# The head of a layered kernel: x loaded in column quarters, the first two weight units multiplied in parts of 128 rows

## The chip, the cores and the metric

One core of a Trainium2 chip runs the kernel. The metric is the device time of one execution in microseconds (us), lower is better; a time shown is the median of several executions.

## The reference

The input x is 256 tokens of width 1024 in 32-bit floats. Three layers with feed-forward blocks follow; this case concerns only how the first one begins:

```python
u = rms_norm(h, norm_mix_g[l])            # (x * rsqrt(mean(x*x) + eps)) * gain
z = u @ w_in[l]                           # [256, 1024] @ [1024, 5640]
qa, ka, va, qk_b, vb, ob, ib, fb, ga, gb = jnp.split(z, IN_SPLITS, axis=-1)
qa = rope(to_heads(qa, A_HEADS), pos)
...
i_pre = (ib + b_igate[l].astype(ib.dtype)).transpose(0, 2, 1)
f_pre = (fb + b_fgate[l].astype(fb.dtype)).transpose(0, 2, 1)
hb = mlstm_chunkwise(to_heads(qb, B_HEADS), to_heads(kb_, B_HEADS), to_heads(vb, B_HEADS), i_pre, f_pre)
```

The eight columns ib and fb (the gates) are kept in a small tensor of their own, `wif`.

## The kernel before

**Units.** All weights stream through three slots of `raw`, one unit of 1 MB at a time. A wide unit is 512 rows by 512 columns: four row blocks (k = 0..3) of 128 rows, each a [128, 512] piece of the slot. Two units make one 512-column stretch of the output. Units 0 and 1 give the columns of qa, units 2 and 3 (`KA`) those of ka, units 4 and 5 (`VA`) va; units 6 to 9 (`QKB`) are narrow ones (256 columns by 1024 rows) for the convolution.

**Each product three times.** A weight w is split into `whi` (ScalarE, a copy that rounds) and `wlo` = w - `whi` (VectorE). x is split likewise into `xhi` and `xlo`. A product is xhi*whi + xhi*wlo + xlo*whi, three matmuls accumulated in PSUM. ScalarE increments `hi_done` with each unit, VectorE `lo_done`; TensorE increments `unit_used` when it is through with one, which lets ScalarE overwrite the slot's `whi`. The queue on SyncE (SP) refills a slot of `raw` when `lo_done` says that it is free.

**x.** x lies with its tokens on the partitions and must be turned: TensorE transposes it in blocks of 128x128 into PSUM banks 4 to 7 (`turn_x`, line 1970), 2 blocks for each of the eight chunks c of 128 columns. ScalarE copies a chunk out times the gain (`turned_gain`, line 680) to `xhi`, VectorE makes `xlo` (line 1054). The factor rsqrt(mean) is applied later, when the results leave PSUM.

**The head, in order.** SP issues x's columns 0 to 511 (one transfer for each of the two row tiles, 256 KB each, `x_full[0]`), then unit 0 as 128 rows, 128 rows and 256 rows, then x's columns 512 to 1023, `wif`, unit 1 in halves, three small ones, and whole units from there on. TensorE runs `idle(8)` (matmuls on zeros, 16 passes), turns the first half of x (8 transposes), runs `idle(6)`, and then `wide_halves(0)`: for each half of a unit 4 matmuls high*high, 4 xlo*whi, 4 xhi*wlo. The second half of x is turned in the middle of unit 0. After unit 0 come the gates' 8 matmuls (line 2039, all of x against `wif`), and unit 1.

**The gates' small work.** VectorE adds the two parts of the gate products (lines 1273, 1275); after unit 1 TensorE selects and turns them (line 2048, `gate_ps` 3), VectorE applies bias and factor (lines 1336 to 1342, `gate_dve` 2), ScalarE takes exp and log (lines 819, 821, with a table load) and after these copies the results of units 0 and 1 out of PSUM (line 808). VectorE then rotates them (`rotate`, lines 1101 to 1105, two row tiles), makes unit 5's `wlo`, and builds the diagonal matrices `diag` (lines 1301 to 1309). TensorE waits for these (`gate_dve` 5) ahead of four matmuls at line 2067, which stand between unit 4 and unit 5.

Every engine works through its own instructions in the order in which they are written; only semaphores tie them together.

Of the kernel before, what the change touches and what calls it, by code (L numbers as in the profile page):

```python
# [15 lines left out]
P = 128  # L16
# [45 lines left out]
TURN_BANKS = {T_MIX: (4, 5, 6, 7), T_Y0: (4, 5, 2, 3), T_M0: (0, 1, 5, 7), T_M1: (0, 1, 5, 7)}  # L62
# [122 lines left out]
def build(nc, t, out):  # L185
# [7 lines left out]
    with ExitStack() as ctx:  # L193
# [154 lines left out]
        quarter_hi, quarter_full = sem("quarter_hi"), sem("quarter_full")  # L348
        half_full = [sem(f"half_full{u}") for u in range(2)]
        half_hi, half_lo = sem("half_hi"), sem("half_lo")  # L350
        x_full = [sem(f"x_full{h}") for h in range(2)]
# [46 lines left out]
        def _(sp):  # L398
# [41 lines left out]
            def half_unit(u, h, s):  # L440
                k = 4 * u + 2 * h
                sp.dma_start(raw[:, u, 1024 * h:1024 * h + 1024].rearrange("p (a b) -> p a b", a=2),
                             cols(w_in, k, 2, 0, 512)).then_inc(s, 16)

            for h in range(2):
                for r in range(RT):
                    v = slice(512 * h, 512 * h + 512)
                    sp.dma_start(res[:, r, v], t["x"][0, r * P:(r + 1) * P, v]).then_inc(x_full[h], 16)
                if h == 0:
                    for k, s in enumerate((quarter_full, half_full[0])):  # L450
                        sp.dma_start(raw[:, 0, 512 * k:512 * k + 512], w_in[P * k:P * k + P, 0:512]).then_inc(s, 16)
                    half_unit(0, 1, raw_full[0])
            sp.dma_start(wif[:, :, :], t["wif"]).then_inc(wif_full, 16)
            half_unit(1, 0, half_full[1])
            half_unit(1, 1, raw_full[1])
# [3 lines left out]
            wide(KA, w_in, 512)  # L459
# [175 lines left out]
        def _(act):  # L635
# [174 lines left out]
            for u in range(PROJ):  # L810
# [3 lines left out]
                if u < PROJ - 1:  # L814
                    hi(u + 3, u % 3)
# [180 lines left out]
        def _(dve):  # L996
# [251 lines left out]

            def lo_half(u, h):
                v = slice(1024 * h, 1024 * h + 1024)  # L1250
                dve.wait_ge(hi_done if h else half_hi, u + 1)
                dve.tensor_tensor(wlo[:, u, v], raw[:, u, v], whi[:, u, v], ALU.subtract)\
                    .then_inc(lo_done if h else half_lo, 1)

            dve.wait_ge(gcol_full, 16)
            dve.wait_ge(quarter_full, 16)
            dve.tensor_copy(whi[:, 0, 0:512], raw[:, 0, 0:512]).then_inc(quarter_hi, 1)
            turned_gain(T_MIX, N_MIX, 0, (0, 1))
            dve.wait_ge(quarter_hi, 1)
            lo_half(0, 0)  # L1260
            turned_gain(T_MIX, N_MIX, 0, (2, 3))
            lo_half(0, 1)
            for h in range(2):
                dve.wait_ge(x_full[h], 16 * RT)
# [32 lines left out]
            for u in range(PROJ):  # L1297
# [22 lines left out]
                if u < 7 and u != 4:  # L1320
                    lo(u + 3)
                elif 7 <= u < 19:
                    scores(u - 7)
# [7 lines left out]
                if u == 0:  # L1331
                    dve.wait_ge(rstd_ready, 2)
                    dve.wait_ge(bias_full, 48)
                    dve.wait_ge(gate_ps, 3)
                    for r in range(RT):
                        ins = dve.scalar_tensor_tensor(out=gates[:, r, :], in0=ps[:, 4, 8 * r:8 * r + 8],
                                                       scalar=rstd[:, r:r + 1], in1=bif[:, :], op0=ALU.mult, op1=ALU.add)
                    ins.then_inc(gate_dve, 1)
                    dve.wait_ge(gate_dve, 1)
                    dve.scalar_tensor_tensor(out=rh(0), in0=f_pre, scalar=-1.0, in1=f_pre, op0=ALU.mult, op1=ALU.max)\  # L1340
                        .then_inc(gate_dve, 1)
                    link(dve.tensor_scalar(rh(72), f_pre, 0.0, None, ALU.min))
# [309 lines left out]
        def _(pe):  # L1652
# [316 lines left out]
            idle(8)  # L1969
            def turn_x(half):  # L1970

                pe.wait_ge(x_full[half], 16 * RT)
                for b in (2 * half, 2 * half + 1):
                    for c in (2 * half + b, 2 * half + b + 2):
                        bank, a = turn_at(T_MIX, c)
                        for r in range(RT):
                            ins = pe.transpose(ps[:, bank, a + P * r:a + P * r + P], res[:, r, P * c:P * c + P], ident)
                    ins.then_inc(tr_ps, 1)

            def wide_halves(u):  # L1980

                for h in range(2):
                    ks = (2 * h, 2 * h + 1)
                    if u == 0 and h == 0:
                        pe.wait_ge(quarter_hi, 1)
                    else:
                        pe.wait_ge(hi_done if h else half_hi, u + 1)
                    for k in ks:
                        pe.wait_ge(xhi_done, KC * T_MIX + 4 * u + k + 1)
                        if u == 0 and k == 1:  # L1990
                            pe.wait_ge(half_hi, 1)
                        for r in range(RT):
                            pe.matmul(ps[:, r, :], x(4 * u + k, P * r, P)[0], w(u, 512 * k, 512)[0],  # L1993
                                      start=u == 0 and k == 0, stop=False)
                    for r in range(RT):
                        for k in ks:
                            if r == 0:
                                pe.wait_ge(xlo_done, KC * T_MIX + 4 * u + k + 1)
                            pe.matmul(ps[:, r, :], x(4 * u + k, P * r, P)[1], w(u, 512 * k, 512)[0], start=False, stop=False)  # L1999
                    pe.wait_ge(lo_done if h else half_lo, u + 1)  # L2000
                    for r in range(RT):
                        for k in ks:
                            ins = pe.matmul(ps[:, r, :], x(4 * u + k, P * r, P)[0], w(u, 512 * k, 512)[1],  # L2003
                                            start=False, stop=u == 1 and k == 3)
                    if u == 0 and h == 0:
                        turn_x(1)
                ins.then_inc(unit_used, 1)
# [3 lines left out]
            idle(6)  # L2011
            tiles = 0
            for u in range(PROJ):
# [7 lines left out]
                if QKB <= u < VB:  # L2021
                    if free(tiles):
                        pe.wait_ge(*free(tiles))
                    narrow(u, u % 3, tiles % 4, turned=turned)
                    tiles += 1
                else:
                    if u < 2:
                        wide_halves(u)
                    else:
# [281 lines left out]
```

## Time and profile before

| | |
|---|---|
| median of 3 runs | 1347.59 us |
| lowest, highest | 1347.57, 1349.1 us |
| span of the profiled execution | 1345.7 us |
| TensorE busy (PE) | 1340.6 us |
| VectorE busy (DVE) | 1049.5 us |
| ScalarE busy (ACT) | 702.4 us |
| GpSimd busy (POOL) | 130.1 us |

The span runs from the first to the last instruction of one profiled execution; the page states no other time for that execution. The median is 1.9 us above the span. Busy times are sums over the span. Starts are counted from the span's start. PE is TensorE's matmuls, PEld its weight loads, SPq and ACTq are the instructions that issue transfers.

### The profile page before, as it was taken

Reading aid. Unit: us, or ns where it says so; the run is one execution under the profiler, and the core shown is the slowest. Engines: PE = TensorE matmul, PEld = TensorE weight load, DVE = VectorE, ACT = ScalarE, POOL = GpSimd, SP = SyncE. Lnnn points to the kernel's source line nnn. Section 1 sums busy time; section 2 is a strip of 40 time slices with the busy share of each in tenths; the row PEclk is TensorE's granted clock in tenths of the full one; section 3 lists DMA queues with packets and bytes.
Section 4 is the critical chain, followed back from the end, with each engine's and each line's share of the span. In section 5 each row is a group of like instructions: output and inputs, shape, how many; then the busy total and the mean of one; then the engine's idle time right before and its main releaser. Section 6 shows DMA issues by size and latency. Waiting matters only on the chain.

```text
span 1345.7 us, 18021 instructions
## 1 busy us (share of the span) xinstructions
PE 1340.6 (100%) x6497; PEld 1110.3 (83%) x6497; DVE 1049.5 (78%) x1802; ACT 702.4 (52%) x937; POOL 130.1 (10%) x158
## 2 busy tenths in 40 slices
PE   9999999999999999999999999999999999999999
PEld 8988888888888888887888888888888888888887
DVE  6994668878868877768778888698887888698775
ACT  5666446444464444577664444544445677644442
POOL 4042000020010000142000000000000432100000
DMA  9644455675555555554346555465556542455552
GB/s 278 211 161 149 166 169 190 235 262 200 200 165 198 199 194 191 172 182 144 126 145 230 187 187 188 156 219 187 187 187 207 169 157 95 149 197 196 200 199 90
DMA packets 108809, 246.30 MB, mean 183 GB/s; under 512 B 5112, under 2 KB 9636, under 8 KB 108624
## 3 DMA queue, kind: packets, MB, share of 16 engines
q1 hardware_dynamic: 106576, 240.19, 52.8%
q0 software_dynamic: 1744, 4.70, 1.2%
q8 instruction: 35, 0.57, 0.2%
q10 hardware_dynamic: 432, 0.66, 0.1%
q14 instruction: 22, 0.18, 0.0%
HBM read 244.45 MB, written 1.07 MB: 182 GB/s over the span
## 4 chain that ended last, share of the span: by engine, by line
PE 98%; DVE 1%; ACT 0%; issue 0%; POOL 0%; DVEq 0%
PE ps L1707 27%; PE ps L1655 17%; PE ps L1657 17%; PE ps L1656 17%; PE ps L1712 13%; PE ps L1904 1%; PE ps L1681 1%; PE ps L1958 1%; PE ps L1942 1%; PE ps L2227 0%; DVE wlo L1512 0%; PE ps L1966 0%; PE ps L1993 0%; PE ps L2003 0%; PE ps L1999 0%
## 5 line engine op out<-in xcount | busy, mean ns | idle before, releaser
L1707 PE MATMUL ps<-whi,xx 128*128 128x512 f32 x1600 | 379.2, 389 | 0.0
L1707 PEld LDWEIGHTS ps<-whi,xx 128*128 128x128 f32 x1600 | 300.4, 188 | 62.2
L1014 DVE TENSOR_TENSOR wlo<-raw,whi 128x2048 fp32r<-128x2048 f32 x120 | 274.7, 2289 | 63.9 <-ACT whi L651 62.5
L651 ACT ACTIVATE whi<-raw 128x2048 fp32r<-128x2048 f32 x120 | 229.1, 1909 | 88.4 <-PE ps L1712 88.4
L1212 DVE STREAM_TRANSPOSE sc<-sc 32x128 f32<-32x128 f32 x784 | 237.5, 303 | 11.7
L643 ACT ACTIVATE whi<-raw 128x2048 fp32r<-128x2048 f32 (+1 forms) x135 | 204.7, 1530 | 73.6 <-PE ps L1657 51.0
L1009 DVE TENSOR_TENSOR wlo<-raw,whi 128x2048 fp32r<-128x2048 f32 x75 | 171.2, 2289 | 45.9 <-ACT whi L643 45.5
L1655 PE MATMUL ps<-whi,hhi 128*128 128x512 f32 (+1 forms) x506 | 199.0, 393 | 0.0
L1712 PE MATMUL ps<-wlo,xx 128*128 128x512 f32 x800 | 197.6, 389 | 0.0
L1657 PE MATMUL ps<-whi,hlo 128*128 128x512 f32 (+1 forms) x506 | 197.0, 389 | 0.0
L1656 PE MATMUL ps<-wlo,hhi 128*128 128x512 f32 (+1 forms) x506 | 196.7, 389 | 0.0
L1655 PE MATMUL ps<-whi,xx 128*128 128x512 f32 x464 | 187.8, 405 | 0.3 <-DVE xx L1530 0.3
L1657 PE MATMUL ps<-whi,xx 128*128 128x512 f32 x464 | 181.7, 391 | 0.0
L1656 PE MATMUL ps<-wlo,xx 128*128 128x512 f32 x464 | 180.9, 390 | 0.0
L1712 PEld LDWEIGHTS ps<-wlo,xx 128*128 128x128 f32 x800 | 150.2, 188 | 31.1
L742 ACT ACTIVATE hhi<-sc 128x512 fp32r<-128x512 f32 x49 | 31.1, 634 | 193.4 <-DVE sc L1212 193.4
L1657 PEld LDWEIGHTS ps<-whi,hlo 128*128 128x128 f32 x506 | 95.0, 188 | 20.0
L1655 PEld LDWEIGHTS ps<-whi,hhi 128*128 128x128 f32 x506 | 95.1, 188 | 19.2 <-DVE hlo L1217 0.4
L1656 PEld LDWEIGHTS ps<-wlo,hhi 128*128 128x128 f32 x506 | 95.2, 188 | 18.7
L1657 PEld LDWEIGHTS ps<-whi,xx 128*128 128x128 f32 x464 | 87.1, 188 | 19.1
L1655 PEld LDWEIGHTS ps<-whi,xx 128*128 128x128 f32 x464 | 87.3, 188 | 17.3 <-issue 1.1
L1656 PEld LDWEIGHTS ps<-wlo,xx 128*128 128x128 f32 x464 | 87.5, 189 | 16.1
(286 smaller groups left out, 1165.8 us busy)
## 6 DMA issues: line engine op xcount, KB each, us to landing
raw<-in_ffn_gate_up SPq DMA_DIRECT2D x88, 1024.0 KB, 5.2
raw<-in_ffn_w_down SPq DMA_DIRECT2D x44, 1024.0 KB, 5.0
raw<-in_w_in SPq DMA_DIRECT2D x40, 1024.0 KB, 5.1
raw<-in_gate_up SPq DMA_DIRECT2D x22, 1024.0 KB, 5.2
raw<-in_w_out SPq DMA_DIRECT2D x12, 1024.0 KB, 4.9
raw<-in_w_down SPq DMA_DIRECT2D x11, 1024.0 KB, 5.0
raw<-in_w_mem_kv SPq DMA_DIRECT2D x4, 1024.0 KB, 5.2
raw<-in_w_proj_a SPq DMA_DIRECT2D x2, 1024.0 KB, 4.9
```

The source lines that it names most:

```text
L643: ins = act.activation(whi[:, slot, v], raw[:, slot, v], ACT.Copy)
L651: act.activation(whi[:, c % 3, :], raw[:, c % 3, :], ACT.Copy).then_inc(hi_done, 1)
L742: act.activation(hhi[:, par, :], hidT, ACT.Copy).then_inc(h_hi, 1)
L1009: dve.tensor_tensor(wlo[:, u % 3, v], raw[:, u % 3, v], whi[:, u % 3, v], ALU.subtract)\
L1014: dve.tensor_tensor(wlo[:, c % 3, :], raw[:, c % 3, :], whi[:, c % 3, :], ALU.subtract)\
L1212: ins = dve.transpose(dst[32 * a:32 * a + 32, :, b, :], src[32 * b:32 * b + 32, :, a, :])
L1655: pe.matmul(o, stat[0], mov[0], start=start, stop=False)
L1656: pe.matmul(o, stat[0], mov[1], start=False, stop=False)
L1657: return pe.matmul(o, stat[1], mov[0], start=False, stop=stop)
L1681: ins = pe.transpose(ps[:, bank, a:a + P], res[:, r, P * c:P * c + P], ident)
L1707: pe.matmul(ps[:, banks[r], :], x(4 * half + k, P * r, P)[part], whi[:, slot, 512 * k:512 * k + 512], start=half == 0 and k == 0 and part ...
L1712: ins = pe.matmul(ps[:, banks[r], :], x(4 * half + k, P * r, P)[0], wlo[:, slot, 512 * k:512 * k + 512], start=False, stop=half == 1 and k ...
```

## The change

x arrives in four column quarters (256 columns of both row tiles, one transfer of 256 KB each). Units 0 and 1 arrive in eight parts of 128 rows, two after each quarter of x. ScalarE and VectorE split each part by itself (`hi_part`, `lo_part`), each behind the chunk of x of the same number. TensorE turns a quarter of x (4 transposes) at a time and goes chunk by chunk: `high` (2 matmuls), `w_low` of the chunk before (2), `x_low` (2), with the next quarter turned ahead of `x_low` in chunks 1, 3 and 5. `idle(8)` becomes `idle(6)` (12 passes), `idle(6)` becomes `idle(2)` (4 passes). Units 2 and 3 arrive and are split in halves, and are multiplied by halves, three matmuls at a time. The gates' 8 matmuls move from behind unit 0 to behind unit 1, their selection (line 2048) from behind unit 1 to behind unit 2; on VectorE bias and factor of the gates come ahead of unit 4's `wlo` instead of behind unit 3's. ScalarE's square of x and its issue of the remaining constants (line 803) follow the last part of unit 1.

```diff
+            def x_part(q):
+                v = slice(256 * q, 256 * q + 256)
+                sp.dma_start(res[:, :, v], t["x"][0].rearrange("(r p) d -> p r d", p=P)[:, :, v]).then_inc(x_full[q], 16)
+
+            def w_part(u, k):
+                row = P * (4 * u + k)
+                sp.dma_start(raw[:, u, 512 * k:512 * k + 512], w_in[row:row + P, 0:512])\
+                    .then_inc(raw_full[u] if k == 3 else part_full[3 * u + k], 16)
+
+            def half_unit(u, h):
+                if u == 3:
+                    sp.wait_ge(lo_done, 1)
+                sp.dma_start(raw[:, u % 3, 1024 * h:1024 * h + 1024].rearrange("p (a b) -> p a b", a=2),
+                             cols(w_in, 4 * (u - KA) + 2 * h, 2, 512, 512))\
+                    .then_inc(raw_full[u % 3] if h else half_full[u - KA], 16)
+
+            for u in range(2):
+                x_part(2 * u)
+                w_part(u, 0)
+                w_part(u, 1)
+                x_part(2 * u + 1)
+                w_part(u, 2)
+                w_part(u, 3)
...
+            half_unit(KA, 0)
+            half_unit(KA, 1)
             sp.dma_start(bif[:, 0:BH], across(t["b_igate"][0])).then_inc(bias_full, 16)
             sp.dma_start(bif[:, BH:2 * BH], across(t["b_fgate"][0])).then_inc(bias_full, 16)
             sp.dma_start(cwr[:, :], t["conv_w"][0].rearrange("j (c p) -> (j c) p", p=P)).then_inc(bias_full, 16)
-            wide(KA, w_in, 512)
+            half_unit(KA + 1, 0)
+            half_unit(KA + 1, 1)
...
+            def hi_part(u, k):
+                act.wait_ge(raw_full[u] if k == 3 else part_full[3 * u + k], 16)
+                v = slice(512 * k, 512 * k + 512)
+                act.activation(whi[:, u, v], raw[:, u, v], ACT.Copy).then_inc(hi_done if k == 3 else part_hi, 1)
+
             def hi_half(u, h):
+                act.wait_ge(raw_full[u % 3] if h else half_full[u - KA], 16 * (u // 3 + 1) if h else 16)
+                if u == 3 and h == 0:
+                    act.wait_ge(unit_used, 1)
                 v = slice(1024 * h, 1024 * h + 1024)
-                if u == 0 and h == 0:
-
-                    v = slice(512, 1024)
-                act.wait_ge(raw_full[u] if h else half_full[u], 16)
-                act.activation(whi[:, u, v], raw[:, u, v], ACT.Copy).then_inc(hi_done if h else half_hi, 1)
+                act.activation(whi[:, u % 3, v], raw[:, u % 3, v], ACT.Copy).then_inc(hi_done if h else half_hi, 1)
 
             act.wait_ge(gcol_full, 16)
-            turned_gain(T_MIX, N_MIX, 0, (0, 1))
-            hi_half(0, 0)
-            turned_gain(T_MIX, N_MIX, 0, (2, 3))
-            hi_half(0, 1)
+            for c in range(KC):
+                act.wait_ge(tr_ps, c // 2 + 1)
+                act.activation(xhi[:, c, :], ps[:, 4 + c % 4, SEQ * (c // 4):SEQ * (c // 4) + SEQ], ACT.Copy,
+                               scale=gain_col(N_MIX, c)).then_inc(xhi_done, 1)
+                if c > 0:
+                    hi_part(c // 4, c % 4)
             act.wait_ge(wif_full, 16)
             act.activation(wifs[:, :, 0:8], wif[:, :, :], ACT.Copy).then_inc(wif_hi, 1)
-            act.wait_ge(x_full[0], 16 * RT)
-            act.wait_ge(x_full[1], 16 * RT)
+            for q in range(4):
+                act.wait_ge(x_full[q], 16)
             act.activation(xn[:, 0, :], res[:, 0, :], ACT.Square, scale=DM ** -0.5, accum_out=ss[:, 0:1]).then_inc(sq_done, 2)
-            turned_gain(T_MIX, N_MIX, 1)
-            hi_half(1, 0)
-            hi_half(1, 1)
             act.dma_start(cst[:, P:C_W], t["consts"][:, P:C_W]).then_inc(cst_full, 16)
-            hi(2, 2)
+            hi_half(KA, 0)
+            hi_half(KA, 1)
 
             def evac(n, dst, r, func=ACT.Copy):
 
@@ -811,7 +828,10 @@
                 if u == 17:
 
                     evac_pT(8)
-                if u < PROJ - 1:
+                if u == 0:
+                    hi_half(KA + 1, 0)
+                    hi_half(KA + 1, 1)
+                elif u < PROJ - 1:
                     hi(u + 3, u % 3)
...
+            for c in range(KC):
+                dve.wait_ge(xhi_done, c + 1)
+                dve.scalar_tensor_tensor(out=xlo[:, c, :], in0=ps[:, 4 + c % 4, SEQ * (c // 4):SEQ * (c // 4) + SEQ],
+                                         scalar=gain_col(N_MIX, c), in1=xhi[:, c, :], op0=ALU.mult, op1=ALU.subtract)\
+                    .then_inc(xlo_done, 1)
+                lo_part(c // 4, c % 4)
+            dve.wait_ge(wif_hi, 1)
+            dve.tensor_tensor(wifs[:, :, 8:16], wif[:, :, :], wifs[:, :, 0:8], ALU.subtract).then_inc(wif_lo, 1)
+            for q in range(4):
+                dve.wait_ge(x_full[q], 16)
             dve.tensor_tensor_reduce(out=xn[:, 1, :], in0=res[:, 1, :], in1=res[:, 1, :], scale=1.0 / DM, scalar=0.0,
                                      op0=ALU.mult, op1=ALU.add, accum_out=ss[:, 1:2]).then_inc(sq_done, 2)
-            dve.wait_ge(wif_hi, 1)
-            dve.tensor_tensor(wifs[:, :, 8:16], wif[:, :, :], wifs[:, :, 0:8], ALU.subtract).then_inc(wif_lo, 1)
-            turned_gain(T_MIX, N_MIX, 1)
-            lo_half(1, 0)
-            lo_half(1, 1)
-            dve.wait_ge(gate_ps, 1)
-            dve.tensor_copy(gate_t, ps[0:16, 4, 0:SEQ]).then_inc(gate_copied, 1)
-            dve.wait_ge(gate_copied, 1)
-            dve.tensor_tensor(gate_t, gate_t, ps[0:16, 4, SEQ:2 * SEQ], ALU.add).then_inc(gate_copied, 1)
-            lo(2)
+            lo_half(KA, 0)
+            lo_half(KA, 1)
+
+            def gate_sums():
+                dve.wait_ge(gate_ps, 1)
+                dve.tensor_copy(gate_t, ps[0:16, 4, 0:SEQ]).then_inc(gate_copied, 1)
+                dve.wait_ge(gate_copied, 1)
+                dve.tensor_tensor(gate_t, gate_t, ps[0:16, 4, SEQ:2 * SEQ], ALU.add).then_inc(gate_copied, 1)
+
+            def gate_inputs():
+                dve.wait_ge(rstd_ready, 2)
...
+                if u == 0:
+                    gate_sums()
+                    lo_half(KA + 1, 0)
+                    lo_half(KA + 1, 1)
+                if u == 1:
+                    gate_inputs()
+                if 0 < u < 7 and u != 4:
                     lo(u + 3)
...
-                if u == 0:
-                    dve.wait_ge(rstd_ready, 2)
-                    dve.wait_ge(bias_full, 48)
-                    dve.wait_ge(gate_ps, 3)
...
-            idle(8)
+            idle(6)
+
+            def turn_x(q):
+
+                pe.wait_ge(x_full[q], 16)
+                for c in (2 * q, 2 * q + 1):
+                    for r in range(RT):
+                        a = SEQ * (c // 4) + P * r
+                        ins = pe.transpose(ps[:, 4 + c % 4, a:a + P], res[:, r, P * c:P * c + P], ident)
+                ins.then_inc(tr_ps, 1)
+
+            def high(c):
+
+                u, k = c // 4, c % 4
+                if c == 0:
+                    pe.wait_ge(quarter_hi, 1)
+                elif k == 3:
+                    pe.wait_ge(hi_done, u + 1)
+                else:
+                    pe.wait_ge(part_hi, k + 3 if u else k)
+                pe.wait_ge(xhi_done, c + 1)
+                for r in range(RT):
+                    pe.matmul(ps[:, r, :], x(c, P * r, P)[0], w(u, 512 * k, 512)[0], start=c == 0, stop=False)
+
+            def x_low(c):
+
+                pe.wait_ge(xlo_done, c + 1)
+                for r in range(RT):
+                    pe.matmul(ps[:, r, :], x(c, P * r, P)[1], w(c // 4, 512 * (c % 4), 512)[0], start=False, stop=False)
+
+            def w_low(c):
+
+                u, k = c // 4, c % 4
+                pe.wait_ge(lo_done if k == 3 else part_lo, u + 1 if k == 3 else 3 * u + k + 1)
+                for r in range(RT):
+                    ins = pe.matmul(ps[:, r, :], x(c, P * r, P)[0], w(u, 512 * k, 512)[1], start=False, stop=c == KC - 1)
+                if k == 3:
+                    ins.then_inc(unit_used, 1)
+
...
+            idle(2)
+            for c in range(KC):
+                high(c)
+                if c > 0:
+                    w_low(c - 1)
+                if c in (1, 3, 5):
+                    turn_x((c + 1) // 2)
+                x_low(c)
+            w_low(KC - 1)
...
-                if u == 0:
+                if u == 1:
 
 
                     pe.wait_ge(wif_lo, 1)
@@ -2039,9 +2096,9 @@
                         ins = pe.matmul(ps[0:16, 4, :], wifs[:, k, :], xx[:, k, :, :].rearrange("p a b -> p (a b)"),
                                         start=k == 0, stop=k == KC - 1)
                     ins.then_inc(gate_ps, 1)
-                if u == 1:
                     pe.wait_ge(bias_full, 48)
                     pe.transpose(ps[:, 5, 0:32], cwr[:, :], ident[0:32, 0:32]).then_inc(gate_ps, 1)
+                if u == 2:
                     pe.wait_ge(cst_full, 16)
                     pe.wait_ge(gate_copied, 2)
                     for r in range(RT):
```

## Rows read from the trace of the kernel before

**Rows 1.** The page: chain of waits by engine, whole span.

```profile
PE 98%; DVE 1%; ACT 0%; issue 0%; POOL 0%; DVEq 0%
```

**Rows 2.** The chain of waits in time, 0 to 60 us: start, length, what.

```profile
1.05 3.79 PE ps L1966 x16
4.84 1.86 PE ps L1977 x8
8.95 0.91 PE ps L1999 x4
10.77 0.87 PE ps L1977 x8
```

**Rows 3.** Timeline of the head: start, length, engine, line, operation, idle before.

```profile
1.64 1.70 PE L1966 MATMUL ps<-pr 128*128 128x128 f32 x7
4.78 1.09 PE L1977 MATMUL ps<-cst,res 128*128 128x128 f32 x4
5.97 0.47 ACT L680 ACTIVATE xx<-ps,gcol 128x256 fp32r<-128x256 f32 x1 [2.81 <-PE ps L1977]
7.10 0.62 ACT L788 ACTIVATE whi<-raw 128x512 fp32r<-128x512 f32 x1
7.62 0.83 ACT L680 ACTIVATE xx<-ps,gcol 128x256 fp32r<-128x256 f32 x2
7.79 1.17 PE L1993 MATMUL ps<-whi,xx 128*128 128x512 f32 x4
7.82 1.23 DVE L1252 TENSOR_TENSOR wlo<-raw,whi 128x1024 fp32r<-128x1024 f32 x1
```

**Rows 4.** Transfers issued in three short windows: KB each, us from issue to landing.

```profile
res<-in_x SPq DMA_DIRECT2D x1, 256.0 KB, 3.1
cst<-in_consts ACTq DMA_DIRECT2D x1, 64.0 KB, 3.3
...
raw<-in_w_in SPq DMA_DIRECT2D x1, 256.0 KB, 4.1
...
raw<-in_w_in SPq DMA_DIRECT2D x1, 512.0 KB, 7.1
```

**Rows 5.** Timeline: when SP issued these.

```profile
0.74 0.86 SPq L448 DMA_DIRECT2D res<-in_x  x2
1.65 0.90 SPq L451 DMA_DIRECT2D raw<-in_w_in  x2
4.59 1.29 SPq L442 DMA_DIRECT2D raw<-in_w_in  x2
```

**Rows 6.** Busy time by windows, 0 to 6.5 us; at the end PEclk, DMA share, GB/s.

```profile
0.00:6.50 6.50, 5.45 (x24) 5.24 (x25) 0.61 (x3) 1.96 (x3) 0.32 (x6) 1.00 0.67 219
```

**Rows 7.** Timeline of the gates' small work, 21 to 37 us.

```profile
21.70 0.59 PE L2048 MATMUL ps<-cst,memT 16*128 16x8 f32 x4
24.72 0.35 DVE L1336 SCALAR_TENSOR_TENSOR small<-ps,rstd,bif 128x8 f32<-128x8 f32 x2
24.94 1.92 ACT L643 ACTIVATE whi<-raw 128x2048 fp32r<-128x2048 f32 x1 [2.45 <-DMA raw<-in_w_in]
25.20 0.17 DVE L1342 TENSOR_SCALAR small<-small 128x8 f32<-128x8 f32 x1
26.76 0.19 ACT L819 ACTIVATE small<-small 128x8 f32<-128x8 f32 x1
28.15 0.48 PE L1655 MATMUL ps<-whi,xx 128*128 128x512 f32 x1
28.37 1.25 ACT L808 ACTIVATE work<-ps,rstd 128x512 f32<-128x512 f32 x2
33.77 2.29 DVE L1009 TENSOR_TENSOR wlo<-raw,whi 128x2048 fp32r<-128x2048 f32 x1
36.91 2.50 DVE L1309 TENSOR_TENSOR turned_a<-cst,small 128x512 fp32r<-128x512 f32 x4
39.47 0.82 PEld L2067 LDWEIGHTS ps<-turned_a,hhi 128*128 128x128 f32 x4
```

More of the change, by code:

```diff
@@ L347, in build @@
         ident_full, warm_ready = sem("ident_full"), sem("warm_ready")
-        quarter_hi, quarter_full = sem("quarter_hi"), sem("quarter_full")
+        quarter_hi = sem("quarter_hi")
+        part_full = [sem(f"part_full{n}") for n in range(6)]
+        part_hi, part_lo = sem("part_hi"), sem("part_lo")
         half_full = [sem(f"half_full{u}") for u in range(2)]
         half_hi, half_lo = sem("half_hi"), sem("half_lo")
-        x_full = [sem(f"x_full{h}") for h in range(2)]
+        x_full = [sem(f"x_full{q}") for q in range(4)]
         raw_full = [sem(f"raw_full{s}") for s in range(3)]
@@ L1247, in _, with lo_part @@
             dve.memset(pr[:, 0, 0:P], 0.0).then_inc(warm_ready, 1)
+            def lo_part(u, k):
+                if u == 0 and k == 0:
+                    dve.wait_ge(quarter_hi, 1)
+                elif k == 3:
+                    dve.wait_ge(hi_done, u + 1)
+                else:
+                    dve.wait_ge(part_hi, k + 1 + 2 if u else k)
+                v = slice(512 * k, 512 * k + 512)
+                dve.tensor_tensor(wlo[:, u, v], raw[:, u, v], whi[:, u, v], ALU.subtract)\
+                    .then_inc(lo_done if k == 3 else part_lo, 1)
@@ L1249, in lo_half @@
             def lo_half(u, h):
+                dve.wait_ge(hi_done if h else half_hi, u + 1 if h else u - KA + 1)
                 v = slice(1024 * h, 1024 * h + 1024)
-                dve.wait_ge(hi_done if h else half_hi, u + 1)
-                dve.tensor_tensor(wlo[:, u, v], raw[:, u, v], whi[:, u, v], ALU.subtract)\
+                dve.tensor_tensor(wlo[:, u % 3, v], raw[:, u % 3, v], whi[:, u % 3, v], ALU.subtract)\
                     .then_inc(lo_done if h else half_lo, 1)
             dve.wait_ge(gcol_full, 16)
-            dve.wait_ge(quarter_full, 16)
+            dve.wait_ge(part_full[0], 16)
@@ L1257, in _ @@
             dve.tensor_copy(whi[:, 0, 0:512], raw[:, 0, 0:512]).then_inc(quarter_hi, 1)
[L1258 to L1264, printed above, removed]
+            for c in range(KC):
[4 more added lines that the diff above has]
+                lo_part(c // 4, c % 4)
@@ new lines, in gate_inputs @@
+            def gate_inputs():
+                dve.wait_ge(rstd_ready, 2)
+                dve.wait_ge(bias_full, 48)
+                dve.wait_ge(gate_ps, 3)
+                for r in range(RT):
+                    ins = dve.scalar_tensor_tensor(out=gates[:, r, :], in0=ps[:, 4, 8 * r:8 * r + 8],
+                                                   scalar=rstd[:, r:r + 1], in1=bif[:, :], op0=ALU.mult, op1=ALU.add)
+                ins.then_inc(gate_dve, 1)
+                dve.wait_ge(gate_dve, 1)
+                dve.scalar_tensor_tensor(out=rh(0), in0=f_pre, scalar=-1.0, in1=f_pre, op0=ALU.mult, op1=ALU.max)\
+                    .then_inc(gate_dve, 1)
+                link(dve.tensor_scalar(rh(72), f_pre, 0.0, None, ALU.min))
@@ L1330, in _ @@
                                       rbc0.unsqueeze(1).to_broadcast([P, 2, SEQ]), ALU.mult).then_inc(cin_done, 1)
-                if u == 0:
-                    dve.wait_ge(rstd_ready, 2)
-                    dve.wait_ge(bias_full, 48)
-                    dve.wait_ge(gate_ps, 3)
[L1335 to L1342, printed above, removed]
                 if u == 1:
@@ L1968, in _ @@
             pe.wait_ge(warm_ready, 1)
-            idle(8)
[L1970 to L1978, printed above, removed]
@@ L1980, in wide_halves @@
-            def wide_halves(u):
-                for h in range(2):
[L1983 to L1994, printed above, removed]
-                    for r in range(RT):
[L1996 to L2006, printed above, removed]
@@ new lines, in x_low @@
+            def x_low(c):
[5 more added lines that the diff above has]
+                pe.wait_ge(lo_done if k == 3 else part_lo, u + 1 if k == 3 else 3 * u + k + 1)
+                for r in range(RT):
+                    ins = pe.matmul(ps[:, r, :], x(c, P * r, P)[0], w(u, 512 * k, 512)[1], start=False, stop=c == KC - 1)
+                if k == 3:
+                    ins.then_inc(unit_used, 1)
@@ L2007, in wide_halves, with halved @@
+            def halved(u, banks):
+                for h in range(2):
+                    pe.wait_ge(lo_done if h else half_lo, u + 1 if h else u - KA + 1)
+                    for r in range(RT):
+                        for k in (2 * h, 2 * h + 1):
+                            ins = three(ps[:, banks[r], :], x(4 * (u - KA) + k, P * r, P), w(u % 3, 512 * k, 512),
+                                        u == KA and k == 0, u > KA and k == 3)
                 ins.then_inc(unit_used, 1)
@@ L2026, in _ @@
                 else:
-                    if u < 2:
-                        wide_halves(u)
-                    else:
+                    if 2 <= u < 4:
+                        halved(u, (tiles % 4, (tiles + 1) % 4))
+                    elif u >= 4:
                         wide(u, u % 2, (tiles % 4, (tiles + 1) % 4), (free(tiles), free(tiles + 1)),
```

20 lines of the change are left out of this document (3 added, 17 removed).

## The prediction
> **What bounds the kernel now.** I read the page's chain of waits first: 98% of it is TensorE, no other engine above 1% [rows 1]. The reader is to see that a matmul removed, or a pause of TensorE, counts at its full length, and that nothing later gives a pause back. The change alters no number of products (48 matmuls for units 0 and 1, 8 for the gates, 24 for each of units 2 and 3), so only three things can move the time: when TensorE starts on real products, whether it pauses once it has started, and at which clock it runs. I then read the chain in time and the timeline of the head. The first product starts at 7.79 [rows 3], and from there on products follow each other at 0.91 / 4 = 0.228 us [rows 2]. Before it lie 16 filler passes, 8 transposes, and fillers again [rows 2]. The most that an earlier start can bring is therefore a part of 7.79 us, and less than 2 us by the sum below, or 0.15% of the time.
>
> My sums are made against the span of 1345.7 us of the profiled execution; the median of the runs is 1.9 us above it, and I add the difference to the median.
>
> **The start.** x's first transfer lands 3.1 us after its issue at 0.74 [rows 4, 5]: 3.84. A column quarter has the same 256 KB in more and shorter pieces; I take 3.9, and bound it by 3.84 and by 4.7, where the second such transfer lands now. The identity matrix, issued at the same time by the other queue, lands after 3.3 us: 4.04 [rows 4]. That one is the later of the two. Fillers: passes start 0.213 apart ((1.70 - 0.42) / 6, a last one's length taken off [rows 3]); 12 of them from 1.05 end at about 3.8. So turning starts at about 4.15 (now 4.84 [rows 2]). Four transposes at 1.86 / 8 = 0.23 take it to 5.05, four filler passes to 5.9. Beside that ScalarE gets the first chunk 0.1 us after the transposes' modelled end, as now (the first four end at 4.78 + 1.09 = 5.87, ScalarE starts at 5.97 [rows 3]): 5.3, plus 0.47 = 5.75. The first part of unit 0, today issued at 1.65 as third 256 KB and there 4.1 us later [rows 4, 5], becomes the second transfer: about 4.8, its rounding about 5.3. First product at 5.9 instead of 7.79: **-1.9 us**. Bounds: 5.75 (the chunk) and 6.7 (if both transfers come a place late).
>
> **What then lies in TensorE's row.** Before, 8 transposes come after the first product, now 12. The 4 more cost 4 x 0.87 / 8 [rows 2] = **+0.45**. Each switch from transposes to products costs some 0.1 (the four products behind one take 1.17 [rows 3], where three steps of 0.228 and a last one of 0.39 make 1.07); there are 2 more: **+0.2**. The first two products fall into the stretch in which transposes still ran at half pace (0.23 against 0.11 each [rows 2]): **+0.4**, between 0 and 0.45.
>
> **New waits in the head.** In chunk 2 `high` needs `xhi` of chunk 2, which needs the quarter turned in chunk 1, and it needs `hi_part` of chunk 2, which stands behind that `xhi` on ScalarE although its weights landed long before. So from the transposes on there is a chain: 0.1 to wake ScalarE, 0.36 until its next instruction (two 0.47 copies of chunks take 0.83 together), 0.62 for a 512-column rounding [rows 3], about 0.05 to TensorE: 1.15 us from the transposes' modelled end. The only work between is `x_low` of chunk 1, 2 x 0.228, of which some 0.1 is already past by then. TensorE stands for 0.8 us. It is the same in chunks 4 and 6, since the turns stand in chunks 1, 3 and 5: 3 x 0.8 = **+2.4**. Bounds: 3 x 0.3, if rounding the part were not in the chain and only the 0.47 copy was, and 3 x 1.0. In chunks without a turn ScalarE needs about 0.36 + 0.55 per chunk against TensorE's 6 x 0.228 = 1.37, VectorE half of 1.23 [rows 3] and a 256-column operation, so both keep up. Landings are not in it: 256 KB now land per 0.7 to 1.1 us (unit 1's last half, the end of 3 MB, is there at about 5.3 + 7.1 = 12.4 [rows 4, 5]), while the last part is wanted only at about 18.
>
> Sum of the head: -1.9 + 0.45 + 0.2 + 0.4 + 2.4 = **+1.55 us** at the end of unit 1. Moving the gates' 8 matmuls costs nothing in TensorE's row. Their inputs are ready: ScalarE's copy of `wif` comes right after the last part of unit 1. Units 2 and 3 by halves: landed by 16, rounded by 22 and wanted at 23, free. SP waits for `lo_done` 1 (unit 0's slot free) ahead of unit 3's halves, as before; behind that wait stand only unit 4 and later, which must wait for later counts anyway. GpSimd's small loads start some 8 us later; nobody asks for them in this stretch.
>
> **The gates' small work.** Counted from the start of unit 3 (28.15), it runs now: selection at 21.70, bias and factor on VectorE 24.72 to 25.37, exp at 26.76, that is 1.39 ahead of unit 3; ScalarE could not be earlier since unit 4's rounding, late by its transfer, lasts until 26.86. Then table load and log, the two copies of the result until 29.62 (2.86 after exp), two rotations on VectorE up to 33.77, unit 5's `wlo`, and the diagonals from 36 to 39.41 [rows 7]. TensorE loads their first weight at 39.47, 0.06 later, where without a wait the load would stand about a tenth of a us earlier. This chain is just hidden: its cover is 0.1 us.
>
> Afterwards the selection comes behind unit 2. Its modelled end then lies about 0.3 before unit 3's start (the 0.36 us of the matmuls at line 2054 follow it); VectorE begins 0.1 later and needs 0.56 until ScalarE may start (24.72 to 25.28): exp at +0.4 instead of -1.39, **1.8 us later**. Unit 4's `wlo` (2.3) runs on VectorE meanwhile and is over before ScalarE's 2.86. Nothing in the rest of the chain gets shorter. TensorE reaches line 2067 at 11.5 after unit 3's start as before, the diagonals come 13.1 after it. With 0.1 of cover that makes **+1.65 us**. Bounds: 0, if some of VectorE's row from 29.6 on was waiting rather than working (I see no pause above 0.1 there), and 2.2. What stands behind it on VectorE moves with TensorE and so keeps its distance.
>
> **The sum.** +1.55 + 1.65 = +3.2 us: span 1348.9, time 1347.59 + 3.2 = **1350.8 us**, 0.24% slower. Its own range is 1349.9 to 1351.9.
>
> **The clock.** The page's PEclk reads 1.00 even for the first 6.5 us [rows 6], yet the transposes at 4.84 take twice as long as those at 10.77 [rows 2]: the engine ran at the lower of its levels (1.2 GHz) until shortly before 6.5, after 5.4 us of nearly gapless fillers, and at 2.4 GHz afterwards. The changed head has a pause of about 0.4 between fillers and transposes. The Trainium skill ("TensorE: Matmul & The Clock Gate", Part 1) says that the engine starts throttled, that activity releases it, and that the moment varies from run to run. This speaks against fewer fillers; the trace shows the late rise but not what a pause does to it.
>
> **Rivals.**
> (a) The clock rises late. From 5.9 to, say, 9.3 us products would take 0.43 instead of 0.23, by the ratio of the two rows of transposes. Half of 3.2 us is lost: +1.6, time 1352.4. For it: the new pause, and 4 fillers in place of 12. Against: the engine is busy for over 80% of the first 6.5 us in either order. 12%.
> (b) The chain of the gates stays hidden, because part of VectorE's row was slack. Then only the head counts: 1347.59 + 1.55 = 1349.1. Against it: 0.06 us between diagonals and weight load. 14%.
> (c) The head's waits do not appear, since ScalarE is woken earlier than I think or the rounding gets ahead: -0.85 for the head, +1.65 for the gates, time 1348.4. Against it: ScalarE's order is fixed in the code. 8%.
> (d) The other side, not slower: the earlier start carries through. The first product at 5.9 decides, and both chains fit under TensorE's work: from the turn to `high` within 0.35 us instead of 1.15 and the diagonals within 11.5 instead of 13.1. Price: -1.9 + 1.05 = -0.85, time 1346.7. It decides as soon as the hand-over is shorter than `x_low`. 4%.
> The forecast has 60%; 2% are left for other things.
>
> **Range and chances.** 0.2% is 2.7 us, about what a measurement of this kernel tells from no change. Slower by more means above 1350.3: most of the forecast's 60% (0.5) and (a) together, 0.61. Faster by more means below 1344.9, out of reach of an earlier start of 1.9 us: 0.02. The rest, 0.37, is within. For 8 in 10 I take the forecast, (a), and half of (b): 1349.0 to 1352.8.
>
> **What would show it.** First product (line of `high`) near 5.9; three pauses of TensorE of 0.8 us, each behind four transposes and two `x_low`, ended by ScalarE's rounding; no pause ended by a transfer. At the end of unit 1 TensorE is 1.5 us later than now. A pause of 1.6 us ahead of the diagonals' matmuls, ended by VectorE; from there on a constant distance of about 3.2 us. Wrong if the products of chunks 2, 4 and 6 follow without a pause, if the diagonals' weights load at once, or if the first products' pace stays at 0.43 beyond 7 us.

## The result, and the profile after

The change made the kernel slower. In the first session the median is 1352.96 us in 8 runs against 1348.03 us in 8 runs before: 4.9 us more. The ratio estimated from all runs is 1.0032, 95% interval 1.0024 to 1.0041, or 4.3 us. The forecast was 1350.8, 3.2 us more than 1347.59, with a range to 1352.8; its direction was right and its size too small. The median lies 0.2 above the top of that range, but the kernel before was 0.4 slower here than when the forecast was made. The 8 runs form two groups, three from 1350.58 to 1351.05 and five from 1352.90 to 1353.14. The profiled execution has a span of 1351.3 us against 1345.7.

The page's chain of waits by engine, kernel after:

```profile
PE 96%; DVE 2%; ACT 1%; issue 1%; DMA 0%; POOL 0%; ACTq 0%; DVEq 0%
```

It stood at 98% TensorE before [rows 1]. Two percentage points of 1351 us are not accurate enough for a sum, but they name the engines: VectorE and ScalarE now stand in the chain. The list of waits in the first 50 us shows where (who waited for whom: us in total, times, longest):

```profile
PEld ps L2031 <- ACT whi L798: 3.2, 3, 1.1
...
PE ps L2031 <- ACT whi L798: 1.9, 3, 0.6
...
PEld ps L2124 <- DVE turned_a L1355: 1.8, 1, 1.8
...
PE ps L2124 <- DVE turned_a L1355: 1.4, 1, 1.4
```

L2031 is `high`, L798 `hi_part`, L2124 the products with the diagonals (L2067 before). Three waits of equal kind, and one. The timeline of the kernel after at the first of the three:

```profile
9.76 1.05 PE L2017 MATMUL ps<-cst,res 128*128 128x128 f32 x4
...
10.47 0.81 PE L2037 MATMUL ps<-whi,xx 128*128 128x512 f32 x2
10.85 0.47 ACT L810 ACTIVATE xx<-ps,gcol 128x256 fp32r<-128x256 f32 x1 [3.90 <-PE ps L2017]
11.22 0.62 ACT L798 ACTIVATE whi<-raw 128x512 fp32r<-128x512 f32 x1
...
11.90 0.73 PE L2031 MATMUL ps<-whi,xx 128*128 128x512 f32 x2 [0.62 <-ACT whi L798]
```

Read it from the turn down: ScalarE copies the chunk 0.04 us after the transposes' modelled end (10.81), rounds the part from 11.22 to 11.84, and `high` starts at 11.90. Between lie only the two low products of 10.47. The other two pauses end at 15.97 and 20.07. The rounding had had its data for about 3 us: the part of the weights was issued at 2.68 and landed 5.3 us later, at 8.0 (ScalarE sat idle for 3.90 before the copy).

The start of the head, from the chain of waits in time (start, length):

```profile
0.74 3.53 DMA res<-in_x
4.41 1.08 PE ps L2017 x4
5.49 0.85 PE ps L2006 x4
6.34 1.06 PE ps L2031 x2
7.40 0.85 PE ps L2037 x2
8.26 0.85 PE ps L2031 x2
9.11 0.85 PE ps L2044 x2
9.96 0.87 PE ps L2017 x4
```

Two products take 0.85, nearly twice the 0.46 of before, and four transposes 0.87, where eight took as much before [rows 2]: TensorE stayed at 1.2 GHz up to about 10.4 us, against 6.5 before. PEclk prints 1.00 for 6.0 to 10.5 us too, so the clock must be read from the pace of equal instructions.

The gates' small work, answering to [rows 7]:

```profile
31.16 0.61 PE L2105 MATMUL ps<-cst,memT 16*128 16x8 f32 x4
31.91 0.36 DVE L1315 SCALAR_TENSOR_TENSOR small<-ps,rstd,bif 128x8 f32<-128x8 f32 x2 [3.36 <-PE ps L2105]
32.50 0.21 ACT L839 ACTIVATE small<-small 128x8 f32<-128x8 f32 x1 [2.57 <-DVE small L1319]
34.14 1.25 ACT L825 ACTIVATE work<-ps,rstd 128x512 f32<-128x512 f32 x2
39.53 2.29 DVE L1029 TENSOR_TENSOR wlo<-raw,whi 128x2048 fp32r<-128x2048 f32 x1
42.68 2.50 DVE L1355 TENSOR_TENSOR turned_a<-cst,small 128x512 fp32r<-128x512 f32 x4
```

The distances from exp to the copies and from unit 5's low part to the diagonals are as before. Only the start hangs on something else: VectorE idles 3.36 us until the selection, ScalarE 2.57 until VectorE. The products with the diagonals, in the timeline of the kernel before and in the chain in time of the kernel after:

```profile
39.63 1.09 PE L2067 MATMUL ps<-turned_a,hhi 128*128 128x512 f32 x4
```

```profile
45.23 1.20 PE ps L2124 x4
```

They start 5.6 us later. The last product before them starts at 43.42 in the kernel after, so the pause is 1.81 - 0.23 = 1.6 us. From 45.23 to the start of TensorE's last matmul it is 1303.1 us, against 1302.9 before: all but 0.1 to 0.2 us of the difference is made in the first 45 us.

### The profile page after: what moved, and what is told of

Read it like the earlier page. It is cut to its first block, busy times and chain, and to the rows that moved or that the text cites. A ratio compares the mean times of both kernels' runs of the same rounds, so it can differ in the third digit from the quotient of the medians.

```text
span 1351.3 us, 18017 instructions
## 1 busy us (share of the span) xinstructions
PE 1342.6 (99%) x6485; PEld 1109.4 (82%) x6485; DVE 1050.2 (78%) x1808; ACT 702.9 (52%) x942; POOL 133.3 (10%) x158
## 4 chain that ended last, share of the span: by engine, by line
PE 96%; DVE 2%; ACT 1%; issue 1%; DMA 0%; POOL 0%; ACTq 0%; DVEq 0%
PE ps L1747 27%; PE ps L1695 17%; PE ps L1697 17%; PE ps L1696 16%; PE ps L1752 13%; PE ps L1944 1%; PE ps L1721 1%; PE ps L1998 1%; PE ps L1982 1%; PE ps L2284 0%; DVE wlo L1552 0%; PE ps L2031 0%; PE ps L2044 0%; DMA res<-in_x 0%; PE ps L1908 0%
## 5 line engine op out<-in xcount | busy, mean ns | idle before, releaser
L656 ACT ACTIVATE whi<-raw 128x2048 fp32r<-128x2048 f32 (+1 forms) x133 | 200.9, 1525 | 69.6 <-PE ps L1697 55.2
```

Source lines behind the costliest of these rows:

```text
L656: ins = act.activation(whi[:, slot, v], raw[:, slot, v], ACT.Copy)
```

## The experiments

All were timed in several rounds beside the kernel before, in three further sessions; the changed kernel itself was timed again in the second of these alone. Of its fourteen runs seven form the lower group, 1350.6 to 1351.4 with a median of 1351.0; "the lower group" below means these. Each run has a profiled span, and the time is 1.7 to 1.9 us above it but for two runs, named below.

**Twelve fillers in the kernel before.**

```diff
-            idle(8)
+            idle(6)
```

> The kernel before with 12 filler passes ahead of the transposes instead of 16, so TensorE pauses for about 0.9 us between them (3.8 to 4.8); nothing else changes. Theory P (the pause among the fillers puts the clock's rise off): the transposes stay at 0.21 each and the first products run at 0.43, the rise comes well after 7 us, as in the changed kernel, and the time is 1 to 2.5 us above before. Rival Q (the moment of the rise is chance from run to run, whatever the fillers do): the profile may show either, and the runs of this kernel and of the kernel before are spread over the same two groups in about the same shares.

Median 1348.85 (11 runs from 1346.90 to 1349.49) against 1347.54 in 33 runs of before: ratio 1.0005, interval 0.9996 to 1.0014, which is not clear of no difference. The single runs say more. Three of its runs lie at or below 1347.55, like 17 of the 33 of before; eight lie at 1348.2 to 1349.5, where before has 2 of 33. Its profile:

```profile
4.72 1.94 PE L1977 MATMUL ps<-cst,res 128*128 128x128 f32 x8 [0.73 <-DMA res<-in_x]
6.45 2.34 PE L1966 MATMUL ps<-pr 128*128 128x128 f32 x12
8.55 0.71 PE L1993 MATMUL ps<-whi,xx 128*128 128x512 f32 x2
```

The twelve fillers (6.45) ran at half pace up to about 8.2 us and took 2.1 us in the chain, where they had taken 1.3; they themselves kept the first product back from 7.79 to 8.55, and the products with the diagonals start 0.8 us later than before (40.43). Theory P foresaw a rise after 7 us, which it got, and half-pace products, which this profile does not show. Q foresaw about the same shares; 8 of 11 against 2 of 33, in one session and with nothing else changed, speak clearly for P. They do not tell whether the pause or the smaller number of fillers does it.

**Only the gates' place moved, in the kernel before.** Products behind unit 1, selection behind unit 2, VectorE's order as in the change:

```diff
-                if u == 0:
+                if u == 1:
                     pe.wait_ge(wif_lo, 1)
...
+                if u == 2:
                     pe.wait_ge(cst_full, 16)
                     pe.wait_ge(gate_copied, 2)
...
```

> The kernel before with only the gates' work moved as in the change: 8 products behind unit 1, selection behind unit 2, bias and factor ahead of unit 4's low part. Theory: the diagonals come 1.8 us later against 0.1 us of cover, so TensorE pauses 1.4 to 1.8 us ahead of the diagonals' matmuls and the time rises by 1.6 us (0.12%). Rival (the pause in the changed kernel comes from the head, not from the gates' place): no pause there and no difference in time.

Median 1349.82 against 1347.54, 2.3 us more; ratio 1.0017, interval 1.0008 to 1.0026. From its list of waits:

```profile
DVE small L1326 <- PE ps L2049: 3.4, 1, 3.4
ACT small L819 <- DVE small L1330: 2.9, 1, 2.9
...
PEld ps L2068 <- DVE turned_a L1305: 1.8, 1, 1.8
```

The pause is the same 1.6 us as in the changed kernel (starts 39.98 and 41.79). So it belongs to the gates' place, not to the head. A second one of 0.4 us, not foreseen, appears between units 0 and 1: the gates' 8 products had covered ScalarE's rounding of unit 1's first half. Its timeline:

```profile
14.39 0.96 PE L1994 MATMUL ps<-whi,xx 128*128 128x512 f32 x3 [0.26 <-ACT whi L788]
```

A third part needs no wait. From the first product to the start of unit 3 it is 21.2 us, where it had been 20.4; without the pause of 0.4 another 0.4 is left. The selection and the small transpose ahead of it stood together behind unit 1, with one gap of TensorE in front of them; now they stand in two places, each with a gap. The prediction had put the move at nothing in TensorE's row.

**Quarters turned earlier, in the changed kernel.**

```diff
             for c in range(KC):
+                if c in (1, 3, 5):
+                    turn_x((c + 1) // 2)
                 high(c)
                 if c > 0:
                     w_low(c - 1)
-                if c in (1, 3, 5):
-                    turn_x((c + 1) // 2)
                 x_low(c)
```

> The changed kernel with each quarter of x turned ahead of the high products of chunks 1, 3 and 5, not behind the low products. ScalarE's chain (wake, copy of the chunk, rounding of the part) takes 1.15 to 1.25 us and then lies beside six products (1.37 us). Theory: the three pauses of 0.8 us go, 2.3 us less than the changed kernel. Rival (the parts' transfers or VectorE are just behind ScalarE): the pauses shrink, but 0.2 to 0.5 us is left at each, ended by another engine or a transfer, 1 us less in all.

Median 1348.38 (nine runs 1347.87 to 1348.52, two at 1350.0 and 1350.2): 2.6 us below the lower group of the changed kernel, which was timed in other sessions. The timeline of TensorE around the place of the first pause:

```profile
7.36 0.60 PE L2017 MATMUL ps<-cst,res 128*128 128x128 f32 x4
7.71 0.71 PE L2031 MATMUL ps<-whi,xx 128*128 128x512 f32 x2
8.26 0.62 PE L2044 MATMUL ps<-wlo,xx 128*128 128x512 f32 x2
8.72 0.63 PE L2037 MATMUL ps<-whi,xx 128*128 128x512 f32 x2
9.19 0.62 PE L2031 MATMUL ps<-whi,xx 128*128 128x512 f32 x2
```

There is no pause at any of the three places, so whatever stands behind ScalarE (VectorE, the parts' transfers) was ready in time. A pause costs a little more than its idle time. From one such `high` to the next, two chunks later, it is 3.22 us here (7.71 to 10.93) and 4.09 in the kernel of the next experiment but one (9.50 to 13.59, both at full pace): 0.87 for each pause, 2.6 for three.

**ScalarE rounds the part before it copies the chunk**, TensorE's order unchanged:

```diff
             for c in range(KC):
+                if c > 0:
+                    hi_part(c // 4, c % 4)
                 act.wait_ge(tr_ps, c // 2 + 1)
...
-                if c > 0:
-                    hi_part(c // 4, c % 4)
```

> The changed kernel with ScalarE rounding each part of the weights ahead of copying the chunk of x of the same number, instead of behind it; TensorE's order is as in the changed kernel. Theory: the 0.55 to 0.6 us of rounding leave the chain between turn and high product and only the copy (0.47) stays, so the three pauses of 0.8 us shrink to about 0.25 each, 1.6 us less than the changed kernel (1349.2 against 1350.8 in the lower group). Rival (VectorE's low parts or the weights' transfers stand right behind ScalarE): the pauses stay above 0.5 us, less than 1 us gained.

Median 1349.93; six runs from 1349.29 to 1350.22, three from 1351.45. The three gaps between starts shrink from 1.01 to 0.59 us, so each pause from 0.79 to 0.36, 1.3 us in all (0.3 us less than forecast). One of the six, 1350.22, has a span of 1347.7, so 2.5 us of its time lie outside the span, 0.7 more than in the others. What is left:

```profile
10.61 0.47 ACT L812 ACTIVATE xx<-ps,gcol 128x256 fp32r<-128x256 f32 x1 [2.60 <-PE ps L2017]
...
11.23 0.70 PE L2031 MATMUL ps<-whi,xx 128*128 128x512 f32 x2 [0.20 <-ACT xx L812]
```

`high` starts 0.15 us after the copy's end instead of 0.06 after the rounding's. Both instructions of ScalarE were in the chain, as the forecast had it.

**The gates' selection in the middle of unit 2**, in the changed kernel:

```diff
+                    if u == KA and h == 0:
+                        pe.wait_ge(cst_full, 16)
+                        pe.wait_ge(gate_copied, 2)
+                        for r in range(RT):
+                            sel = pe.matmul(ps[:, 4, 8 * r:8 * r + 8], ...)
+                        sel.then_inc(gate_ps, 1)
...
```

The selection behind unit 2 is left out in return.

> The changed kernel with the gates' selection between the halves of unit 2 instead of behind it. Exp on ScalarE then follows unit 4's rounding at about 30 instead of 32.5. Theory: the diagonals are there before TensorE wants them, the pause of 1.6 us ahead of their matmuls goes, 1.6 us less than the changed kernel. Rival (VectorE has too much work in that stretch, the chain of the gates only looks like the cause): VectorE's idle time moves but the diagonals come at the same time, under 0.5 us less.

Median 1349.32 (eight runs 1348.94 to 1349.47, three from 1350.76): 1.7 us below the lower group of the changed kernel. VectorE and TensorE at the diagonals:

```profile
37.83 2.50 DVE L1355 TENSOR_TENSOR turned_a<-cst,small 128x512 fp32r<-128x512 f32 x4
```

```profile
41.08 0.39 PE L1697 MATMUL ps<-whi,xx 128*128 128x512 f32 x1
41.30 0.40 PE L2124 MATMUL ps<-turned_a,hhi 128*128 128x512 f32 x1
```

The diagonals are done at 40.33, one us before they are wanted, and the products follow each other at 0.22. Nothing is left of the pause.

**The changed kernel once more.**

> The changed kernel once more, on the chip of the next three. Theory: the clock's rise falls at different moments of the head from run to run; its runs fall into two groups about 2 us apart (near 1350.8 and 1353.0), with products at half pace from 6.2 to about 10.4 in the upper one. Rival: the upper group is a property of the chip of the first measurement and is not seen here.

Six runs in a later session: four from 1350.72 to 1351.35, two at 1352.76 and 1353.04; median 1351.21, before 1347.68, ratio 1.0030 (1.0017 to 1.0042). This time the profile caught an early rise of the clock:

```profile
5.03 0.61 PE L2006 MATMUL ps<-pr 128*128 128x128 f32 x4
5.94 0.70 PE L2031 MATMUL ps<-whi,xx 128*128 128x512 f32 x2 [0.30 <-ACT xx L810]
...
8.39 0.66 PE L2017 MATMUL ps<-cst,res 128*128 128x128 f32 x4 [0.39 <-DMA res<-in_x]
```

Same program, same instructions; four fillers in 0.61 instead of 1.06, full pace from 4.7 us, the first product at 5.94. The upper group appears on this chip too, which refutes the rival. In this profile the diagonals' products start at 43.51 against 45.23, 1.7 us earlier; some of the gain from the pace went into a new wait: the second quarter of x, issued at 2.22, landed only 6.1 us later and kept the turn back by 0.5. This is a pause ended by a transfer, which the prediction had ruled out. The span is 1349.5.

**Sixteen fillers in the changed kernel.**

```diff
-            idle(6)
+            idle(8)
```

> The changed kernel with 16 filler passes instead of 12 ahead of the first transposes: no pause between them, transposes at 4.8 instead of 4.4. Theory P (a pause among the fillers makes the late rise likelier): hardly any run in the upper group, median 0.4 us above the lower group of the changed kernel. Rival Q (chance alone): the same share of runs in the upper group as the changed kernel beside it.

Four runs from 1350.82 to 1351.23, then 1351.91 and 1353.36; median 1351.19. By its time the last one seems to belong to the upper group, but its span is 1349.7, and 3.7 us of its time lie outside the span, 1.8 more than in the others. The six spans run from 1349.0 to 1350.1; the two upper runs of the changed kernel beside it have 1351.0 and 1351.2. So by the span no run is in the upper group. The profile has no pause ahead of the transposes and full pace from about 4.4 us (the sixteen passes take 3.61 us instead of the 3.79 of before [rows 2]). P foresaw this, but 0 of 6 against 2 of 6 is too few to tell it from chance.

**Both reorderings together, with 16 and with 14 fillers.**

> The changed kernel with 16 filler passes, quarters turned ahead of the high products and the gates' selection in the middle of unit 2. Theory: the terms add up, -2.4 and -1.6 against the lower group of the changed kernel, +0.4 for the later transposes: 0.2 to 0.6 us below the kernel before. Rival: the gate chain, once it is earlier, meets another wait (unit 4's rounding, late by its transfer), and 0.5 to 1 us of the pause ahead of the diagonals comes back; then no gain over before.

> The same with 14 filler passes, which end just before the transposes can start. Theory: the first product at 5.9 to 6.2, 0.6 to 1.0 us below the kernel before in its lower group of runs, with few runs in an upper group. Rival: any shortening of the fillers brings runs of the upper group, 1.5 to 2 us above, and the median is no better than with 16.

Medians 1346.94 and 1346.92 (11 runs each, highest 1347.73 and 1347.16) against 1347.68 in 23 runs of before: ratios 0.9994 (0.9985 to 1.0003) and 0.9993 (0.9984 to 1.0002). Neither is clear of no difference, though the medians are 0.7 and 0.8 us lower. No run is in an upper group, and in neither profile does TensorE wait for the diagonals; with 16 fillers the second quarter of x came late and cost 0.5. The profile of the one with 14 fillers:

```profile
5.22 0.69 PE L2006 MATMUL ps<-pr 128*128 128x128 f32 x4
6.15 0.70 PE L2031 MATMUL ps<-whi,xx 128*128 128x512 f32 x2 [0.24 <-ACT xx L810]
6.69 0.62 PE L2037 MATMUL ps<-whi,xx 128*128 128x512 f32 x2
7.15 0.60 PE L2017 MATMUL ps<-cst,res 128*128 128x128 f32 x4
7.50 0.71 PE L2031 MATMUL ps<-whi,xx 128*128 128x512 f32 x2
```

Its diagonals' products start at 38.91, 0.7 us before those of the kernel before (39.63). This is what the earlier start is worth once both chains lie under TensorE's work: 1.6 us at the first product (6.15 against 7.79), less 0.9 for four more transposes, the switches and the gates' small matmuls in two places.

## Why the prediction was right, and where its size was off

**The frame** held: TensorE's row is the time, and a pause is not given back. In all eleven profiles 1302.9 to 1303.1 us lie between the start of the diagonals' products and that of the row's last matmul.

**The start**: forecast 5.9; measured 6.21 in the first profile, 5.94 in the second (there four fillers at full pace made up for a late landing). x's quarter landed 3.5 us after its issue instead of the 3.1 that a piece of the same size had taken, so the turn began at 4.41, not 4.15.

**TensorE's row**: forecast +0.65, measured +0.95 (from the first product to unit 3 it is 21.3 us in the kernel whose quarters are turned earlier, which has no pauses in between, against 20.4 before). Of this 0.4 is the gates' small matmuls, put at nothing and measured in the kernel before with only this part moved; the rest, 0.5, is the four transposes and the switches. That no transfer would end a pause failed in two of the eleven profiles (0.5 us each, the second quarter of x).

**The three pauses**: forecast 0.8 each, measured 0.79 each (gaps of 1.01 less a step of 0.23), 0.87 each with the slower step behind them. Turning earlier removes all of them; ScalarE's order alone removes half.

**The gates' chain**: forecast 1.65, measured 1.6, in the changed kernel and in the kernel before with only this part moved. The tight distance in [rows 7] was the cover, and it was gone.

**The clock** is the term that was mis-sized. The step put the first two products at half pace, +0.4, up to 0.45. In the profiled execution eight products (6.21 to 9.76) ran at 0.427 instead of 0.228, and the second turn took 0.87 instead of 0.44: +2.0 us. The profile with the selection moved, where the clock rose at 4.8, agrees:

```profile
5.88 0.70 PE L2031 MATMUL ps<-whi,xx 128*128 128x512 f32 x2 [0.27 <-ACT xx L810]
...
9.50 0.73 PE L2031 MATMUL ps<-whi,xx 128*128 128x512 f32 x2 [0.62 <-ACT whi L798]
```

From the first product to the end of the first pause it takes 3.62 us, the changed kernel 5.69 (6.21 to 11.90): 2.1 more. Taken together, -1.6 for the start, +0.95 for TensorE's row, +2.1 for the pace, +2.6 for the pauses and +1.6 for the gates make +5.6 (before rounding 5.63), against 45.23 - 39.63 = 5.6 measured. A pace of 0.43 beyond 7 us was also one of the prediction's own signs of being wrong, and it occurred in the first profile.

Rival (a) named this mechanism with 12% and 1352.4 us; the upper group lies at 1353.0 with 5 of the first 8 runs and 2 of 6 in the repeat. Both profiles kept from an upper group show a late rise (10.4 and 9.9), the four kept from a lower group of the same kernel or of one with a single edit an early one (4.4 to 6.4), and the groups of the changed kernel are 2.0 us apart, as much as the pace costs. The forecast of 1350.8 is the lower group, 1350.6 to 1351.4. That it fits so well is in part luck: there the +0.4 for the pace did not occur, and the pauses and TensorE's row cost 0.5 more than forecast. Each group had half of the fourteen runs, and the forecast should have named two times.

The prediction read one rise, at 6.5 us, from one profile and treated it as the kernel's. In the eleven profiles it lay at about 4.4, 4.7, 4.8, 5.4, 6.2, 6.3, 6.4, 6.5, 8.2, 9.9 and 10.4. The same program shows 4.7 and 10.4. Products that start at 6.2 lose half of the distance from there to the rise, 2.1 us for 10.4. The 28 filler passes of the kernel before do not hide a late rise: with the rise at 8.2 instead of 6.5 the first product came 0.8 later. Yet 31 of its 33 runs in one session lie within 1.3 us (1346.88 to 1348.16), so late rises seem rarer there. By the Trainium skill, "TensorE: Matmul & The Clock Gate", Part 1, the moment varies between runs of one kernel; the two profiles of the changed kernel agree. It also says that the cost of the ramp is below 1% of a typical kernel's span and that one should not fit to a specific count of slow matmuls: 2.1 of 1351 us is 0.16% here, but as large as anything else in this change.

**Rivals (b), (c) and (d)** are refuted for this kernel: the pause ahead of the diagonals (1.6) and the three in the head (0.79 each) are all there. (d) needed both chains to fit under TensorE's work; the last two kernels make them fit, and get 1346.9 where (d) said 1346.7.

**Left open**: what makes a late rise likelier. Runs of an upper group came in kernels of the changed kind with 12 fillers and a pause of 0.3 to 0.6 us ahead of the first transposes (7 of 14, 2 of 11, 3 of 11, 3 of 9), and by the span in none of the 28 runs with 14 or 16 fillers and no such pause. In the kernel before, 12 fillers and a pause of 0.7 gave 8 of 11 runs at 1348.2 or above, against 2 of 33. So fewer fillers with a pause behind them go with late rises. Fillers and pause were never changed apart from each other, so the runs do not show which of the two counts, and why the same program rises early in one run and late in the next stays open.

## What to carry to other kernels

An operand that arrives earlier is worth what the slowest hand-over behind it leaves: count, from the producer's last instruction to the consumer, every instruction that the middle engine has in its order between them, and the consumer's own work beside it. Put the producer a step ahead, and what has its data already ahead of what waits. A block that is moved was somebody's cover: look up which small chain starts from it, and how much distance that chain has at its end. Where real work is moved into the first microseconds, read the clock from several executions. And where times form groups, look at the span of each run before a group is explained: one of the slow times here had a fast span.

## What was not expected of the hardware

The moment at which TensorE reaches full pace differed by 5.7 us between two executions of one program (4.7 and 10.4 us after the span's start), while the profile's clock column read 1.00 throughout. And 256 KB of x in pieces of 1 KB, issued at 2.2 us, landed 5.0 us later in one execution and 6.1 in another of the same program.
